# Candidates moved by a two-scalar operation, and a tile's eight diagonal matrices of maxima made in one product

## The chip, the core and the metric

The kernel runs on one core of a Trainium2 chip. A core has TensorE (matrix products, with its weight loads shown apart), VectorE, ScalarE, GpSimd and SyncE (which issues most of the DMAs), each with a program of its own; they meet at semaphores only. The metric is the device time of one execution in microseconds (us), lower being better.

## The reference, cut to what matters

One layer of a streaming encoder runs over 2048 prompt frames and 32 sample frames. Each frame is normalised and projected; half of the projection goes through a pooling mixer, the other half through sparse attention with 8 query heads of 64 on 2 key heads. For every query an indexer scores all visible keys, the 256 best are kept, and softmax attention runs over those:

```python
score = jnp.where(vis[None], score, -jnp.inf)
_, sel = lax.top_k(score, topk)
...
logits = jnp.einsum('bqgrd,bqkgd->bqgrk', qg, ks) * ATTN_SCALE + bias
p = jax.nn.softmax(logits, axis=-1)
```

Both halves are gated, projected out, normalised and added to the input.

## The kernel before, in words

The queries are cut into 17 tiles of 128 (16 of the prompt, the last with the 32 sample frames). The kernel has two phases, one after the other. `phase1` makes the projections, the pooling and the index scores, from a list of steps that all engines walk through. `phase2` is the attention: step t of its loop holds the logits and the weighted values of tile t, the maxima of the logits of tile t+1, the search for a later tile, and the output projection of tile t-2. `pe_step`, `dve_step` and `act_step` merge these series into one order for each engine by given fractions of a step.

**The search.** The 256th best score of each query is found by halving an interval, not by sorting. A query has its own partition and its own candidate `cand`, a column of 128 x 1. A round (`halve`, lines 336 to 355) has three VectorE instructions, each waiting for the one before it: count the scores that reach the candidate (L345, as wide as the tile has keys; it reads the candidate as a scalar per partition), compare the count with 256 and scale the answer to 0 or the width of the interval (L349, one column), and move the candidate (L352, one column). Tiles 2 to 5 are searched in the first phase, 26 rounds each (104). For tiles 6 to 16 ScalarE does 16 rounds in the second phase and VectorE the other 10 (110). Lists of scores are searched one at a time here, so each call has a single candidate column.

**The diagonals.** For each tile, TensorE multiplies queries and keys, and VectorE takes the maximum of each row and head (`maximum`, L1711). `set_shift` (lines 1714 to 1722) turns the eight negated maxima of a query, `nmax`, into eight diagonal matrices in bf16, `shift`: the identity, each row scaled by that query's value, one instruction a head (L1721). TensorE adds them to the logits by a product with ones (L1618), so the first logits of a tile wait for `shift_done`. GpSimd multiplies the exponentials of the nearer keys by the bias (L1501) in the meantime, and ScalarE makes those exponentials (L1576).

After `set_shift` VectorE goes on with `choose` (lines 358 to 386), which makes the mask of a later tile.

Of the kernel before, what the change touches and what calls it, by code (L numbers as in the profile page):

```python
# [16 lines left out]
ALU = mybir.AluOpType  # L17
# [9 lines left out]
P = 128  # L27
# [11 lines left out]
NH, HD, NKV, GRP = 8, 64, 2, 4  # L39
# [37 lines left out]
def key_tiles(t):  # L77
    return t + 1 if t < NPT else PAST // P + 1
# [236 lines left out]
def half_width(r):  # L315
    return 2.0 ** -r
# [9 lines left out]
def recentre(dve, done, n, B, scores):  # L326
    m = len(scores)
    dve.wait_ge(done, n)
    for i, s in enumerate(scores):
        dve.tensor_scalar(s, s, B.cand[:, i:i + 1], None, ALU.subtract).then_inc(done, 1)  # L330
    dve.wait_ge(done, n + m)
    dve.memset(B.cand[:, 0:m], 0.0).then_inc(done, 1)
    return n + m + 1


def halve(dve, done, n, B, scores, first, last):


    m = len(scores)
    for r in range(first, last):  # L340
        if r == ZOOM_AT:
            n = recentre(dve, done, n, B, scores)
        dve.wait_ge(done, n)
        for i, s in enumerate(scores):
            dve.tensor_scalar((B.above, B.reach)[i][:, 0:s.shape[1]], s, B.cand[:, i:i + 1], None,  # L345
                              ALU.is_ge, ALU.add, accum_out=B.cnt[:, i:i + 1]).then_inc(done, 1)
        n += m
        dve.wait_ge(done, n)
        dve.tensor_scalar(B.side[:, 0:m], B.cnt[:, 0:m], TOPK - 0.5, 2.0 * half_width(r), ALU.is_ge, ALU.mult)\  # L349
           .then_inc(done, 1)  # L350
        dve.wait_ge(done, n + 1)
        dve.scalar_tensor_tensor(B.cand[:, 0:m], B.side[:, 0:m], half_width(r), B.cand[:, 0:m], ALU.subtract, ALU.add)\  # L352
           .then_inc(done, 1)
        n += 2
    return n


def choose(dve, done, n, B, i, s):


    def link(ins):
        nonlocal n
        ins.then_inc(done, 1)
        n += 1

    half = half_width(ALL_ROUNDS - 1)
    col = slice(i, i + 1)
    w = s.shape[1]
    dve.wait_ge(done, n)
    link(dve.tensor_scalar(B.lo[:, col], B.cand[:, col], half, None, ALU.subtract))  # L370
    link(dve.tensor_scalar(B.hi[:, col], B.cand[:, col], half, None, ALU.add))
    dve.wait_ge(done, n)
    link(dve.tensor_scalar(B.above[:, 0:w], s, B.hi[:, col], None, ALU.is_gt, ALU.add, accum_out=B.cnt[:, col]))
    link(dve.tensor_scalar(B.reach[:, 0:w], s, B.lo[:, col], None, ALU.is_ge))
    dve.wait_ge(done, n)

    link(dve.tensor_scalar(B.room[:, col], B.cnt[:, col], -1.0, float(TOPK), ALU.mult, ALU.add))

    link(dve.tensor_tensor_scan(s, B.reach[:, 0:w], B.above[:, 0:w], 0.0, ALU.add, ALU.subtract))  # L379
    link(dve.tensor_tensor(B.above[:, 0:w], B.reach[:, 0:w], B.above[:, 0:w], ALU.add))  # L380
    dve.wait_ge(done, n)

    link(dve.scalar_tensor_tensor(B.reach[:, 0:w], s, B.room[:, col], B.above[:, 0:w],  # L383
                                  ALU.is_gt, ALU.is_ge))
    dve.wait_ge(done, n)
    return n
# [830 lines left out]
def phase2(nc, A, sb, sem, identf, identb, onesb, k2, home, loaded, unit, xs, first_q, banks, wide, q_dram, gb_dram, ma_dram,  # L1217
           s_dram, m_dram, g_dram, k_dram):

    def chunks(t):  # L1220
        n = key_tiles(t) * P
        return [(a, min(a + 512, n)) for a in range(0, n, 512)]
# [24 lines left out]
    def last_fl(t, kv=NKV - 1):  # L1247
        return fl[t, kv, key_tiles(t) - 1]
# [17 lines left out]
    def sslot(t):  # L1266
        return (t - FIRST) % 3
# [36 lines left out]
    with ExitStack() as st:  # L1304
# [7 lines left out]
        B = Search(sb, st, 1, SEQ)  # L1312
# [12 lines left out]
        shift = sb(st, "shift", [P, 2, NH, P], BF16)  # L1325
# [5 lines left out]
        nmax = sb(st, "nmax", [P, NH], F32)  # L1331
# [25 lines left out]
        shift_done = sem("shift_done")  # L1357
# [9 lines left out]
        with nc.Block() as block:  # L1367
# [301 lines left out]
            @block.vector  # L1669
            def _(dve):  # L1670
                n = 0

                def link(ins):
                    nonlocal n
                    ins.then_inc(dk, 1)
                    n += 1

                def continue_search(u):

                    nonlocal n  # L1680
                    dve.wait_ge(halved, HALVED * (u - FIRST + 1))
                    dve.tensor_scalar(B.cand[:], minus_cand[:, u % 2:u % 2 + 1], -1.0, None, ALU.mult)\
                       .then_inc(cand_taken, 1)
                    dve.wait_ge(cand_taken, u - FIRST + 1)

                def set_mask(u):
                    nonlocal n
                    w = key_tiles(u) * P
                    if u > FIRST:
                        dve.wait_ge(mask_done, u - FIRST)  # L1690
                    n = choose(dve, dk, n, B, 0, S[sslot(u)][:, 0:w])
                    dve.wait_ge(fl_full, last_fl(u - 3) + 1)
                    dve.tensor_scalar(mask[:, u % 3, 0:w], B.reach[:, 0:w], MASKED, None, ALU.mult)\
                       .then_inc(mask_done, 1)
                    dve.memset(B.room[:], 0.0).then_inc(S_used, 1)

                def maximum(t, h, c):

                    if h == 0 and c == 0:
                        if t < TOPK // P:  # L1700
                            dve.wait_ge(plain_mask, 2 * (t + 1))
                        elif t in EARLY:
                            dve.wait_ge(mask_in[t % 3], 16 * ((t - EARLY[0]) // 3 + 1))
                        else:
                            dve.wait_ge(mask_done, t - FIRST + 1)
                    k = fx[t, h, c]
                    a, b = chunks(t)[c]
                    dve.wait_ge(fx_full, k + 1)
                    if k >= 2:
                        dve.wait_ge(fx_free, k - 1)  # L1710
                    dve.tensor_tensor_reduce(junk[:, k % 2, 0:b - a], max_banks[k % 3][:, 0:b - a], mask[:, t % 3, a:b],  # L1711
                                             1.0, LEAST, ALU.add, ALU.max, mxp[:, h, c:c + 1]).then_inc(fx_free, 1)

                def set_shift(t):
                    dve.wait_ge(fx_free, last_fx(t) + 1)
                    link(dve.tensor_reduce(nmax[:], mxp[:, :, 0:len(chunks(t))], AX.X, ALU.max, negate=True))
                    dve.wait_ge(dk, n)
                    if t >= 2:
                        dve.wait_ge(fl_full, last_fl(t - 2) + 1)
                    for h in range(NH):  # L1720
                        ins = dve.tensor_scalar(shift[:, t % 2, h, :], identb[:], nmax[:, h:h + 1], None, ALU.mult)  # L1721
                    ins.then_inc(shift_done, 1)

                def invert_sums(t):
                    dve.wait_ge(sums_out, 4 * (t + 1))
                    n = GRP * queries(t)
                    dve.reciprocal(den[:, t % 2, 0:n], den[:, t % 2, 0:n]).then_inc(recip_done, 1)  # L1727

                def post_norm(t):
                    nonlocal n  # L1730
                    dve.wait_ge(o_free, 4 * (t + 1))
                    link(dve.tensor_tensor(root[:, 3:4], ss2[:, t, 0:1], ss2[:, t, 1:2], ALU.add))
                    dve.wait_ge(dk, n)
                    n = inverse_root(dve, dk, n, root[:, 0:1], root[:, 1:2], root[:, 2:3], root[:, 3:4], 1.0 / D)
                    dve.wait_ge(gpost_in, 16)
                    dve.scalar_tensor_tensor(osb[:, t % 2], osb[:, t % 2], root[:, 1:2], gpost[:], ALU.mult, ALU.mult)\
                       .then_inc(post_done, 1)

                for t in range(-1, NT + 3):
                    for kind, *at in dve_step(t):  # L1740
                        if kind == "R":
                            u, r = at
                            if r == ZOOM_AT:
                                continue_search(u)
                            n = halve(dve, dk, n, B, [S[sslot(u)][:, 0:key_tiles(u) * P]], r, r + 1)
                        elif kind == "M":
                            maximum(*at)
                        elif kind == "S":
                            set_shift(*at)
                        elif kind == "I":  # L1750
                            invert_sums(*at)
                        elif kind == "P":
                            post_norm(*at)
                        else:
                            set_mask(*at)
# [72 lines left out]
```

## Time and profile before

| | us |
|---|---|
| median of 3 runs | 1680.02 |
| lowest and highest of them | 1678.92, 1682.78 |
| span of the profiled execution | 1677.7 |
| TensorE busy | 1556.8 |
| VectorE busy | 1214.6 |
| ScalarE busy | 892.7 |
| GpSimd busy | 474.5 |

The span is the time from the first to the last instruction of one profiled execution; that execution's time is given by its span alone, and the median stands beside it. Busy times are of whole engines over the whole span, so they hide that the two phases have different limits.

### The profile page before, as it was taken

The page shows a single profiled execution, that of the slowest core. Times are in us where ns is not written, and L with a number is a line of the kernel's source. Part 1 is how long each engine was busy: PE and PEld are TensorE (multiplying, and loading weights), DVE is VectorE, ACT ScalarE, POOL GpSimd, SP SyncE. Part 2 cuts the span into 40 slices and gives each one's busy share as a digit, 9 for nine tenths or more (in the row PEclk, how much of TensorE's full clock was granted, in tenths as well). Part 3 has the DMA queues.
Part 4 walks back from the last instruction along what each step waited for, and adds up shares of the span by engine and source line. Part 5 has one row for each costly group of instructions (what it writes and reads, how often), then busy time and mean ns, then how long its engine had stood idle before and what let it go on. Part 6 is the DMA issues. An engine that isn't in the chain of part 4 may idle for free.

```text
span 1677.7 us, 17799 instructions
## 1 busy us (share of the span) xinstructions
PE 1556.8 (93%) x5191; PEld 869.7 (52%) x5191; DVE 1214.6 (72%) x2940; ACT 892.7 (53%) x1684; POOL 474.5 (28%) x384
## 2 busy tenths in 40 slices
PE   7999899989999999896988898999999999999996
PEld 4555555555555887663444444444444444455552
DVE  5412578779897566675469999999998999985322
ACT  3112333343334455451498988898988776523331
POOL 0111211121113132303343443434323342322241
PEclk9999999989999999987998999999999999999999
DMA  9322322221112111078324211221220220201011
GB/s 366 74 42 49 80 61 71 56 82 40 61 42 70 48 50 37 35 222 253 81 63 120 80 50 57 59 85 39 61 76 26 52 63 1 63 25 26 32 34 49
DMA packets 91979, 120.76 MB, mean 72 GB/s; under 512 B 17150, under 2 KB 63806, under 8 KB 91499
## 3 DMA queue, kind: packets, MB, share of 16 engines
q1 hardware_dynamic: 90506, 115.44, 22.1%
q10 hardware_dynamic: 1376, 4.19, 2.2%
q8 instruction: 42, 0.69, 0.2%
q14 instruction: 55, 0.44, 0.1%
HBM read 76.06 MB, written 43.54 MB: 71 GB/s over the span
## 4 chain that ended last, share of the span: by engine, by line
PE 23%; DVE 18%; ACT 6%; issue 5%; POOL 2%; POOLq 0%; DVEq 0%; ACTq 0%
PE wide L1648 7%; PE wide L1633 7%; DVE above L345 6%; DVE max_junk L1711 3%; ACT act_junk L1542 2%; PE bank L1613 2%; PE bank L1614 2%; PE bank L1615 2%; PE bank L1618 2%; POOL E L1501 1%; PE bank L1599 1%; DVE den L1727 1%; ACT E L1576 1%; DVE reach L383 1%; DVE S L379 1%
## 5 line engine op out<-in xcount | busy, mean ns | idle before, releaser
L931 PE MATMUL bank<-hT,home 128*128 128x512 f32 (+2 forms) x1280 | 486.1, 516 | 5.1 <-DVE sga L1145 2.4
L1501 POOL TENSOR_TENSOR E<-E,home 128x512 f32<-128x512 f32 (+1 forms) x174 | 251.9, 1452 | 446.8 <-ACT E L1576 446.7
L931 PEld LDWEIGHTS bank<-hT,home 128*128 128x128 f32 x1280 | 234.8, 191 | 165.1 <-issue 144.0
L1576 ACT ACTIVATE E<-bank 128x512 f32<-128x512 f32 (+1 forms) x290 | 165.5, 571 | 245.1 <-PE bank L1618 243.3
L1633 PE MATMUL wide<-E,home 128*128 128x512 f32 x544 | 285.1, 606 | 9.9 <-POOL E L1501 9.7
L907 ACT ACTIVATE relu<-wide 128x1024 f32<-128x1024 f32 (+7 forms) x192 | 153.9, 802 | 216.7 <-PE wide L949 154.5
L1183 DVE SCALAR_TENSOR_TENSOR S<-relu,wi,S 128x1024 f32<-128x1024 f32 (+7 forms) x168 | 173.7, 1034 | 100.1 <-ACT relu L907 92.6
L1711 DVE CUSTOM_DVE_ANT_0 max_junk<-bank,mask 128x512 bf16<-128x512 f32 (+3 forms) x230 | 136.9, 615 | 69.2 <-PE bank L1599 54.6
L1648 PE MATMUL wide<-home 128*128 128x512 f32 x272 | 142.2, 614 | 23.2 <-ACT osb L1568 23.0
L1542 ACT ACTIVATE act_junk<-S,minus_cand 128x1152 bf16<-128x1152 f32 (+5 forms) x105 | 155.4, 1480 | 1.5
L949 PE MATMUL wide<-kiT,qiT 96*128 96x512 f32 (+3 forms) x304 | 139.4, 527 | 6.6 <-ACT relu L907 6.5
L931 PE MATMUL bank<-home,hT 128*128 128x296 f32 (+1 forms) x544 | 141.0, 405 | 2.5 <-ACT hT L815 2.5
L1648 PE MATMUL wide<-home,yT 128*128 128x512 f32 x272 | 135.8, 593 | 0.0
L1633 PEld LDWEIGHTS wide<-E,home 128*128 128x128 f32 x544 | 104.4, 194 | 55.6 <-POOL E L1501 17.6
L744 POOL TENSOR_TENSOR win<-U 128x512 f32<-128x512 f32 (+11 forms) x20 | 22.6, 1129 | 347.9 <-ACT U L851 347.9
L931 PEld LDWEIGHTS bank<-home,hT 128*128 128x128 f32 x544 | 104.7, 195 | 30.6 <-ACT hT L815 4.4
L345 DVE TENSOR_SCALAR_CACHE_REDUCE above<-S,search 128x1152 bf16<-128x1152 f32 (+5 forms) x70 | 118.6, 1694 | 0.5
L1615 PE MATMUL bank<-identb,mask 128*128 128x512 bf16 (+1 forms) x290 | 112.8, 389 | 0.0
L1613 PE MATMUL bank<-first_q,k 128*128 128x512 f32 x182 | 107.5, 591 | 5.0 <-issue 2.9
L1618 PE MATMUL bank<-shift,onesb 128*128 128x512 bf16 (+1 forms) x290 | 109.6, 378 | 0.0
L1599 PE MATMUL bank<-k,first_q 128*128 128x512 f32 (+3 forms) x145 | 91.5, 656 | 14.6 <-DVE mxp L1711 9.8
L1711 DVE CUSTOM_DVE_ANT_0 max_junk<-wide,mask 128x512 bf16<-128x512 f32 (+3 forms) x114 | 65.4, 574 | 38.9 <-PE wide L1599 21.4
(204 smaller groups left out, 2392.2 us busy)
## 6 DMA issues: line engine op xcount, KB each, us to landing
xs<-x_prompt SPq DMA_DIRECT2D x16, 512.0 KB, 4.5
home<-w_in SPq DMA_DIRECT2D x16, 512.0 KB, 12.8
xr<-x_prompt SPq DMA_DIRECT2D x16, 512.0 KB, 4.2
y_prompt<-osb SPq DMA_DIRECT2D x16, 512.0 KB, 2.9
first_q<-q_high_scratch SPq DMA_DIRECT2D x24, 256.0 KB, 5.0
s_scratch<-S SPq DMA_DIRECT2D x11, 512.0 KB, 2.7
first_q<-q_low_scratch SPq DMA_DIRECT2D x18, 256.0 KB, 4.2
gb<-gb_scratch SPq DMA_DIRECT2D x17, 256.0 KB, 5.3
```

Source lines behind the costliest of these rows:

```text
L345: dve.tensor_scalar((B.above, B.reach)[i][:, 0:s.shape[1]], s, B.cand[:, i:i + 1], None, ALU.is_ge, ALU.add, accum_out=B.cnt[:, i:i + 1]). ...
L907: act.activation(relu[:, k % 2, 0:b - a], wide[k % 2][:, 0:b - a], ACT.Relu)\
L931: mm = pe.matmul(out, stationary(c), moving(c), start=(c == 0), stop=(c == DC - 1))
L1183: dve.scalar_tensor_tensor(row, relu[:, k % 2, 0:b - a], w, row, ALU.mult, ALU.add)\
L1501: pool.tensor_tensor(E[:, k % 4, :, 0:n], E[:, k % 4, :, 0:n], EB[:, kv * GRP:(kv + 1) * GRP, off:off + n], ALU.mult)\
L1542: act.activation(act_junk[:, 0:w], S[sslot(u)][:, 0:w], ACT.Sign, bias=minus_cand[:, u % 2:u % 2 + 1], accum_out=act_sum[:])\
L1576: act.activation(E[:, k % 4, :, 0:n], banks[2 + k % 2][:, 0:GRP * n].rearrange("p (j n) -> p j n", j=GRP), ACT.Exp).then_inc(fl_free, 1)
L1615: pe.matmul(bank, mask[:, t % 3, kt * P:(kt + 1) * P], identb[:, 0:n].rearrange("p (a n) -> p a n", a=1).broadcast_to([P, GRP, n]), start= ...
L1618: pe.matmul(bank, onesb[:], shift[:, t % 2, kv * GRP:(kv + 1) * GRP, 0:n], start=False, stop=True)\
L1633: pe.matmul(wide[0][:, kv * 512:kv * 512 + GRP * n].rearrange("p (j n) -> p j n", j=GRP), values[:, kt, kv:kv + 2, :].rearrange("p a d -> ...
L1648: mm = pe.matmul(wide[1][:, 0:512], stat, wout[:, c, i * 512:(i + 1) * 512], start=(c == 0), stop=(c == DC - 1))
L1711: dve.tensor_tensor_reduce(junk[:, k % 2, 0:b - a], max_banks[k % 3][:, 0:b - a], mask[:, t % 3, a:b], 1.0, LEAST, ALU.add, ALU.max, mxp[: ...
```

## The change

In a round of the search, the instruction that moves the candidate, (side - half) + candidate, reads two tensors, `side` and `cand`. It becomes a `tensor_scalar` that reads one tensor, `side`, adds the candidate as a scalar per partition, and subtracts the half width as an immediate; one instruction for each candidate column, of which there is one. The order of the two additions changes; the count of instructions and waits does not.

In `set_shift`, the eight scalings of the identity become one `tensor_tensor` product of 128 x 1024: the identity repeated over the heads, times the maxima repeated over the columns.

```diff
@@ -349,9 +349,10 @@
         dve.tensor_scalar(B.side[:, 0:m], B.cnt[:, 0:m], TOPK - 0.5, 2.0 * half_width(r), ALU.is_ge, ALU.mult)\
            .then_inc(done, 1)
         dve.wait_ge(done, n + 1)
-        dve.scalar_tensor_tensor(B.cand[:, 0:m], B.side[:, 0:m], half_width(r), B.cand[:, 0:m], ALU.subtract, ALU.add)\
-           .then_inc(done, 1)
-        n += 2
+        for i in range(m):
+            dve.tensor_scalar(B.cand[:, i:i + 1], B.side[:, i:i + 1], B.cand[:, i:i + 1], half_width(r), ALU.add, ALU.subtract)\
+               .then_inc(done, 1)
+        n += 1 + m
     return n
 
 
@@ -1717,9 +1718,9 @@
                     dve.wait_ge(dk, n)
                     if t >= 2:
                         dve.wait_ge(fl_full, last_fl(t - 2) + 1)
-                    for h in range(NH):
-                        ins = dve.tensor_scalar(shift[:, t % 2, h, :], identb[:], nmax[:, h:h + 1], None, ALU.mult)
-                    ins.then_inc(shift_done, 1)
+                    dve.tensor_tensor(shift[:, t % 2], identb[:].rearrange("p (a n) -> p a n", a=1).broadcast_to([P, NH, P]),
+                                      nmax[:].rearrange("p (h a) -> p h a", a=1).broadcast_to([P, NH, P]), ALU.mult)\
+                       .then_inc(shift_done, 1)
```

## Rows read from the trace of the kernel before

**Rows 1.** The page's first line: the span.
```profile
span 1677.7 us, 17799 instructions
```
**Rows 2.** Who TensorE waited for, 180 to 520 us: us in total, times, longest.
```profile
...
PE bank L1004 <- DVE xs L1069: 0.6, 1, 0.6
...
```
**Rows 3.** Busy us of each engine (xinstructions) by stretch; TensorE's granted clock.
```profile
core 0: us, PE busy (x) PEld busy (x) DVE busy (x) ACT busy (x) POOL busy (x), PEclk, DMA share, GB/s
...
957.00:1302.00 345.00, 318.91 (x994) 156.96 (x993) 330.03 (x748) 299.14 (x552) 133.34 (x88) 0.99 0.19 57
1302.00:1530.00 228.00, 214.43 (x695) 107.30 (x694) 207.56 (x427) 132.25 (x244) 79.64 (x45) 1.00 0.14 38
...
```
**Rows 4.** Who TensorE waited for, 957 to 1302 us.
```profile
PE bank L1599 <- DVE mxp L1711: 13.0, 10, 2.7
...
PE wide L1599 <- DVE mxp L1711: 4.9, 3, 2.7
PE wide L1633 <- POOL E L1501: 2.8, 4, 1.2
```
**Rows 5.** Who TensorE waited for, 1302 to 1530 us.
```profile
PE wide L1633 <- POOL E L1501: 6.7, 6, 1.7
PE bank L1599 <- DVE mxp L1711: 3.6, 5, 1.1
PE wide L1599 <- DVE mxp L1711: 3.1, 4, 2.0
```
**Rows 6.** Two lines of a round: shortest/median/longest ns, first and last start us.
```profile
L352 DVE SCALAR_TENSOR_TENSOR search<-search,search x214: 158/159/1445, 183.6 to 1516.9; 128x1 f32<-128x1 f32 x107
...
L349 DVE TENSOR_SCALAR search<-search x214: 153/153/156, 183.4 to 1516.7; 128x1 f32<-128x1 f32 x107
```
**Rows 7.** Timeline of VectorE and GpSimd, 1195 to 1205 us: start, duration, instruction.
```profile
1198.62 1.02 DVE L352 SCALAR_TENSOR_TENSOR search<-search,search 128x1 f32<-128x1 f32 x1
...
1202.95 0.16 DVE L352 SCALAR_TENSOR_TENSOR search<-search,search 128x1 f32<-128x1 f32 x1
...
1198.34 1.28 POOL L1501 TENSOR_TENSOR E<-E,home 128x512 f32<-128x512 f32 x1 [1.19 <-ACT E L1576]
```
**Rows 8.** Busy us of L352 alone by stretch, with its count.
```profile
180.00:520.00 340.00, 24.87 (x104) 0.98 0.22 61
768.00:957.00 189.00, 7.17 (x20) 0.91 0.42 121
957.00:1302.00 345.00, 18.39 (x60) 0.99 0.19 57
1302.00:1530.00 228.00, 8.43 (x30) 1.00 0.14 38
```
**Rows 9.** L345 in 1178 to 1224 us; two groups of VectorE: busy us, mean ns.
```profile
L345 DVE TENSOR_SCALAR_CACHE_REDUCE above<-home,search x10: 1933/1943/1947, 1178.4 to 1220.2; 128x1664 bf16<-128x1664 f32 x10
...
L1069 DVE TENSOR_SCALAR xs<-xs,small 128x1024 f32<-128x1024 f32 x17 | 12.8, 753 | 0.6
...
L1078 DVE TENSOR_SCALAR home<-home,gpre 128x552 f32<-128x552 f32 x8 | 3.8, 504 | 0.7 <-DMA home<-w_in 0.7
```
**Rows 10.** Timeline of VectorE and GpSimd at three tiles' diagonals.
```profile
1518.56 1.39 DVE L1721 TENSOR_SCALAR shift<-identb,nmax 128x128 bf16<-128x128 bf16 x8
...
1293.82 2.42 DVE L1721 TENSOR_SCALAR shift<-identb,nmax 128x128 bf16<-128x128 bf16 x8 [0.25 <-DVE nmax L1716]
...
1294.25 1.29 POOL L1501 TENSOR_TENSOR E<-E,home 128x512 f32<-128x512 f32 x1 [1.73 <-ACT E L1576]
...
1224.06 2.32 DVE L1721 TENSOR_SCALAR shift<-identb,nmax 128x128 bf16<-128x128 bf16 x8
```
**Rows 11.** Busy us of L1721 alone by stretch, with its count.
```profile
957.00:1302.00 345.00, 13.34 (x48) 0.99 0.19 57
1302.00:1530.00 228.00, 6.14 (x24) 1.00 0.14 38
```
**Rows 12.** A product of 1024 columns on VectorE: busy us, mean ns.
```profile
L1084 DVE TENSOR_TENSOR home<-home,gpre 128x1024 f32<-128x1024 f32 x16 | 18.7, 1215 | 0.0
```
**Rows 13.** Timeline of VectorE and GpSimd, and the chain of waits, 790 to 800 us.
```profile
792.12 4.26 DVE L1721 TENSOR_SCALAR shift<-identb,nmax 128x128 bf16<-128x128 bf16 x8
...
791.81 3.70 POOL L1501 TENSOR_TENSOR E<-E,home 128x512 f32<-128x512 f32 x3
...
795.20 1.28 issue
```

## The prediction

> **What bounds the kernel now.** I read the page first, then the busy time by stretch, then the waits of TensorE in each stretch, and last the two lines of the change in the timeline beside GpSimd. The span is 1677.7 us [rows 1]; the median of the runs shown is 1680.02 us, so 2.3 us lie around the span, and I add them at the end.
>
> The span falls into parts. Up to 768 us runs the projection phase, where TensorE sets the pace: in 180 to 520 us, which holds all 104 search rounds of that phase, it waited for VectorE only once, for 0.6 us [rows 2]. From 768 us on the attention phase runs. In its middle, 957 to 1302 us, VectorE is busy 330.03 of 345 us and TensorE 318.91 [rows 3]. TensorE therefore stands still for 26.1 us there, and 13.0 + 4.9 = 17.9 us of that are waits for VectorE's maxima [rows 4]: VectorE is the bound and TensorE is close behind it. In 1302 to 1530 us TensorE stands still for 13.6 of 228 us [rows 3], 6.7 us of it for VectorE and 6.7 us for GpSimd's bias product [rows 5]. From 957 to 1530 us nine tiles' diagonals and 90 search rounds are made (60 and 30 by stretch); between 768 and 957 us there are 20 rounds, while ScalarE does its own half of the first searches.
>
> **The candidate's step.** Of the 214 executions of L352 half take 0.159 us, but the longest takes 1.445 us. The comparison just ahead of it, L349, has the same one column and takes 0.153 to 0.156 us in all 214 [rows 6]. The timeline says why: the L352 at 1198.62 us lasts 1.02 us and ends at 1199.64, just as the GpSimd product of 1198.34 + 1.28 us ends; the L352 at 1202.95 us meets no GpSimd work and takes 0.16 us [rows 7]. L352 reads two tensors from SBUF and stands until GpSimd has finished; L349 reads one and never stands. What this standing is worth follows by stretch [rows 8]: 18.39 - 60 x 0.159 = 8.85 us in 957 to 1302; 8.43 - 30 x 0.159 = 3.66 us in 1302 to 1530; 24.87 - 104 x 0.159 = 8.33 us in the projection phase.
>
> The new instruction reads one tensor, and the candidate as a scalar per partition. No row shows this form at one column. What bounds it: L345 reads the same candidate the same way, at 1933 to 1947 ns for ten executions of one tile, so that read alone stands for nothing [rows 9]. As to duration, two one-tensor operations with such a scalar take 753 ns at 1024 columns and 504 ns at 552, that is 0.5275 ns a column, which leaves 504 - 551 x 0.5275 = 213 ns at one column [rows 9]. That is 0.054 us over L352's 0.159 us. It is the upper end; the lower end is nothing, where the instruction behind starts before this one has ended. In the attention phase mostly a maximum follows that does not wait for the candidate, so I take 0.03 us a round, between the two: 1.8 us in the middle stretch (0 to 3.2) and 0.9 us in the later one (0 to 1.6). In the projection phase the next comparison often waits for the candidate, so up to 104 x 0.054 = 5.6 us of the 8.3 us go back. Whatever is left there I cost at nothing: TensorE's projections cover it, and all that could come back is the 0.6 us of [rows 2]. If that cover were gone, the 2.7 us would be paid out in full.
>
> **The diagonals.** Eight instructions undisturbed take 1.39 us (the tile at 1518.56). At 1293.82 they take 2.42 us, and GpSimd's product starts only at 1294.25, behind the first of them: it gets in between two of the eight. At 1224.06 they take 2.32 us, with the standing ahead of the first [rows 10]. In the middle stretch 13.34 - 6 x 1.39 = 5.0 us are standing [rows 11]. Two of its six tiles are of the first sort (at 994.82 and 1293.82, 2.1 us), four of the other (2.9 us). One product reads two tensors, so the 2.9 us ahead of it stay; nothing can get into the middle of it, so the 2.1 us go. Its own price has a close row: a product of two f32 tensors of 1024 columns, one of them broadcast along its inner dimension, takes 1.215 us on the mean [rows 12]. That is 0.175 us less than the eight. Saved in the middle stretch: 6 x 0.175 + 2.1 = 3.1 us, or 1.05 us if the standing only moves ahead. In the later stretch, 6.14 - 3 x 1.39 = 1.97 us are standing [rows 11], 1.03 us of it in the middle of the eight (at 1365.16): saved 3 x 0.175 + 1.03 = 1.56 us, at least 0.53.
>
> A rule of the Trainium skill speaks against this part: VectorE: DVE Perf Modes, section "The TRN2 errata", gives 58 cycles plus the columns over the mode's factor at 0.96 GHz, by which eight narrow scalings in the fourfold mode would be an estimated 0.75 us and one product at the single rate 1.13 us, dearer by 0.38 us a tile. By that the whole would come to 1672.6 us. The trace disagrees on the eight, 1.39 us, so I go by the rows.
>
> One tile more counts. At 792.12 us the eight take 4.26 us, since GpSimd has three products in a row and two of them get in between [rows 13]. One product would stand for the first alone (0.92 us) and be done 4.26 - 0.92 - 1.215 = 2.1 us sooner. The chain has 1.28 us there in which TensorE does nothing [rows 13], because its logits wait for this diagonal. I take 1.3 us (0 to 2.1). In the rest of 768 to 957 us I take nothing: ScalarE's comparisons cover it, and without that cover 7.17 - 20 x 0.159 = 4.0 us would be there [rows 8].
>
> **The sum.** Middle stretch: 8.85 - 1.8 + 3.1 = 10.15 us off VectorE. Of TensorE's idle time there 17.9 of 26.1 us are waits for VectorE, so I count 0.7: 7.1 us. Later stretch: 3.66 - 0.9 + 1.56 = 4.3 us, and 6.7 of 13.6 us make it 0.5: 2.2 us. With 1.3 us at 792, 10.6 us. 1677.7 - 10.6 + 2.3 = 1669.4 us. What is late next is TensorE itself, and behind it GpSimd's products. If all came through at the best ends, it would be 11.95 + 5.2 + 2.1 + 0.6 = 19.9 us, or 1660 us.
>
> **Rivals.**
> A: The new one-column step stands for GpSimd like the old. Then it brings no gain and costs its 0.03 us: (3.1 - 1.8) x 0.7 + (1.56 - 0.9) x 0.5 + 1.3 = 2.5 us, 1677.5 us. For it: the diagonals read one tensor as well, and they stand [rows 10]. Against it: L349, one column, and L345, the same scalar, never do [rows 6, 9]. Chance 0.06. The Trainium skill puts it so (GPSIMD Engine Reference, section "Key points"): GpSimd contends with VectorE instructions in a two-port mode or with two SBUF inputs; whether one column counts as such a mode it doesn't say, and L349 says no.
>
> B: The freed time is taken up by TensorE, busy 318.91 of 345 us [rows 3], and by ScalarE, busy 299.14. If 0.2 of it comes through and nothing at 792: 0.2 x (10.15 + 4.3) = 2.9 us, 1677.1 us. Against it: the 17.9 us of waits on VectorE [rows 4]. Chance 0.13.
>
> C: The product is dearer than the eight. Its second operand is broadcast; if that halves the rate of its row, it takes 1.215 us less a fixed 0.159, doubled, plus 0.159, which is 2.27 us, 0.88 us over the eight. Then (8.85 - 1.8 + 2.1 - 5.3) x 0.7 + (3.66 - 0.9 + 1.03 - 2.6) x 0.5 + 1.1 = 4.4 us, 1675.6 us. Against it: the row has such a broadcast too [rows 12]. Chance 0.05.
>
> D, the other side: GpSimd is kept out. Today it gets in after one of the eight; behind the product its bias products come late by up to 1.215 us, and TensorE's weighted values wait for them (2.8 and 6.7 us now [rows 4, 5]). If that hits all nine tiles from 957 us on and all of it reaches TensorE, it costs 10.9 us against the candidate step's (8.85 - 1.8) x 0.7 + (3.66 - 0.9) x 0.5 = 6.3 us: 1684.6 us. It decides from eight of the nine tiles on. Against it: only three of those nine tiles have GpSimd coming in behind the start. Chance 0.04.
>
> **How the numbers follow.** The forecast has 0.72; its own range is 1663 to 1676 us. Within 0.2% (3.4 us, about what a measurement of this kernel can tell from no change) lie A, most of B and a little of the forecast: 0.19. Slower is D: 0.04. Faster has the rest, 0.77. For 8 in 10 the range reaches from 1662, short of the best ends, to 1678, which takes in A, B and C.
>
> **What would show it.** L352 at about 0.16 to 0.22 us in all 214, none near 1 us. L1721 once a tile, 1.2 us or 1.2 us plus one standing. VectorE's busy time down by some 20 to 30 us in all. TensorE's waits for the maxima in the middle stretch down from 17.9 to under 12 us. The forecast is wrong if L352 still shows 1 us records, if TensorE's busy share goes past 97% in the middle with the span unmoved, or if its waits for GpSimd's products grow by several us. A lower granted clock than the 0.99 of that stretch [rows 3] would hide the gain too.

## The result, and the profile after

The median fell from 1680.14 to 1661.53 us (4 runs each); the ratio is 0.9889 with a 95% interval of 0.9875 to 0.9903. The forecast was 1669.4 us and a range of 1662 to 1678 us, so the direction came out, the time lies 0.5 us below the range, and the gain of 18.6 us is 1.75 times the 10.6 us forecast. The profiled execution has a span of 1660.2 us, 17.5 us less than before.

Two of the first lines of the page of the changed kernel, to set beside [rows 1]; the second has the busy time and the count of instructions of each engine:

```profile
span 1660.2 us, 17680 instructions
...
PE 1553.8 (94%) x5191; PEld 871.6 (52%) x5191; DVE 1190.2 (72%) x2821; ACT 892.4 (54%) x1684; POOL 481.3 (29%) x384
```

The 119 instructions that are gone are the seven scalings saved at each of the 17 tiles. VectorE is busy 24.4 us less, TensorE 3 us less.

The candidate's step and the diagonals of the changed kernel, and last the eight scalings of the kernel before; shortest/median/longest ns, beside [rows 6] and [rows 10]:

```profile
L353 DVE TENSOR_SCALAR search<-search,search x214: 212/214/216, 182.9 to 1499.4; 128x1 f32<-128x1 f32 x107
...
L1721 DVE TENSOR_TENSOR shift<-identb,nmax x17: 1224/1226/2224, 769.9 to 1574.9; 128x1024 bf16<-128x1024 bf16 x17
...
L1721 DVE TENSOR_SCALAR shift<-identb,nmax x136: 235/245/1376, 767.9 to 1593.4; 128x128 bf16<-128x128 bf16 x136
```

None of the 214 candidate steps stands any more: the longest takes 0.216 us where it took 1.445. In the timelines 29 of the 110 new steps of the attention phase lie wholly inside one GpSimd instruction and take no longer for it; of the old ones none did. The product takes 1.224 us, and up to 2.2 us with standing ahead of it.

To see where the time came from I cut both traces at the starts of `nmax`, the reduction just ahead of each tile's diagonals, so a stretch runs from one tile's `nmax` to a later one's. The start of tile 0's is also the border of the two phases. The lines of both kernels by stretch (busy us of each engine, then TensorE's granted clock); of the kernel before first, the phases and four stretches of the attention phase:

```profile
0.00:767.70 767.70, 724.55 (x2571) 456.20 (x2571) 501.41 (x1284) 284.82 (x509) 141.27 (x159) 0.98 0.28 83
767.70:1677.70 910.00, 832.20 (x2620) 413.51 (x2620) 713.17 (x1657) 607.92 (x1175) 333.21 (x226) 0.97 0.22 63
...
855.00:898.80 43.80, 38.68 (x111) 18.65 (x110) 33.44 (x99) 39.53 (x89) 16.64 (x13) 0.92 0.29 79
898.80:945.30 46.50, 42.13 (x125) 20.30 (x125) 44.85 (x110) 44.09 (x94) 21.22 (x16) 0.96 0.32 91
...
945.00:1293.00 348.00, 321.72 (x1004) 158.38 (x1004) 333.18 (x749) 303.00 (x562) 135.17 (x87) 0.99 0.21 61
1293.00:1518.00 225.00, 211.43 (x684) 105.60 (x683) 204.42 (x426) 137.07 (x254) 76.12 (x44) 1.00 0.14 38
```

And the same of the changed kernel:

```profile
0.00:769.70 769.70, 729.74 (x2571) 460.70 (x2571) 498.64 (x1283) 285.26 (x509) 141.40 (x159) 0.97 0.28 83
769.70:1660.20 890.50, 824.05 (x2620) 410.88 (x2620) 691.59 (x1538) 607.13 (x1175) 339.93 (x226) 0.98 0.22 64
...
854.40:895.80 41.40, 36.04 (x114) 17.70 (x114) 31.85 (x92) 39.64 (x90) 17.02 (x13) 1.00 0.26 70
895.80:939.50 43.70, 38.99 (x120) 18.99 (x118) 42.23 (x102) 42.25 (x91) 19.76 (x16) 1.00 0.38 109
...
939.70:1277.00 337.30, 319.19 (x1006) 157.22 (x1005) 323.06 (x708) 303.85 (x562) 138.59 (x88) 0.99 0.22 63
1277.00:1501.00 224.00, 212.62 (x685) 106.59 (x684) 199.91 (x405) 136.65 (x254) 79.25 (x44) 0.99 0.14 38
```

The projection phase is 2.0 us longer, the attention phase 19.5 us shorter (910.0 to 890.5). Of those 19.5 us, 2.3 come between the diagonals of tiles 4 and 5 (43.8 to 41.4), 2.8 in the next stretch (46.5 to 43.7), 10.6 in the six tiles behind it (348.1 to 337.5, a little wider than the windows shown) and 1.1 in the three after (225.0 to 223.9); 2.5 us more come at the tile of 792 us (28.6 to 26.1 between its `nmax` and the next). VectorE's busy time in the six tiles falls from 333.18 to 323.06, by 10.1 us: there the run became shorter by about as much as VectorE was relieved. TensorE's busy time in the attention phase fell too, from 832.20 to 824.05 us for the same 2620 instructions, at a granted clock of 0.98 after 0.97; how much of the gain goes with that is taken up at the single tiles below.

### The profile page after: what moved, and what is told of

Its sections match the earlier page's. It is cut to its first block, busy times and chain, and to the rows that moved or that the text cites. A ratio compares the mean times of both kernels' runs of the same rounds, so it can differ in the third digit from the quotient of the medians.

```text
span 1660.2 us, 17680 instructions
## 1 busy us (share of the span) xinstructions
PE 1553.8 (94%) x5191; PEld 871.6 (52%) x5191; DVE 1190.2 (72%) x2821; ACT 892.4 (54%) x1684; POOL 481.3 (29%) x384
## 4 chain that ended last, share of the span: by engine, by line
PE 23%; DVE 20%; issue 6%; ACT 3%; POOL 2%; POOLq 0%; DVEq 0%; ACTq 0%
PE wide L1649 7%; DVE above L345 7%; PE wide L1634 7%; DVE max_junk L1712 3%; PE bank L1614 2%; PE bank L1615 2%; PE bank L1616 2%; PE bank L1619 2%; DVE den L1728 2%; POOL E L1502 2%; PE bank L1600 1%; ACT act_junk L1543 1%; DVE reach L384 1%; DVE S L380 1%; DVE above L381 1%
## 5 line engine op out<-in xcount | busy, mean ns | idle before, releaser
L1502 POOL TENSOR_TENSOR E<-E,home 128x512 f32<-128x512 f32 (+1 forms) x174 | 258.6, 1491 | 423.6 <-ACT E L1577 423.6
L1649 PE MATMUL wide<-home 128*128 128x512 f32 x272 | 140.0, 605 | 24.1 <-ACT osb L1569 23.9
L932 PE MATMUL bank<-home,hT 128*128 128x296 f32 (+1 forms) x544 | 144.6, 413 | 2.5 <-ACT hT L816 2.5
L345 DVE TENSOR_SCALAR_CACHE_REDUCE above<-S,search 128x1152 bf16<-128x1152 f32 (+5 forms) x70 | 118.6, 1695 | 0.5
L1600 PE MATMUL bank<-k,first_q 128*128 128x512 f32 (+3 forms) x145 | 92.3, 661 | 10.6 <-DVE mxp L1712 5.8
```

The lines of the kernel that those rows point to most:

```text
L932: mm = pe.matmul(out, stationary(c), moving(c), start=(c == 0), stop=(c == DC - 1))
L1502: pool.tensor_tensor(E[:, k % 4, :, 0:n], E[:, k % 4, :, 0:n], EB[:, kv * GRP:(kv + 1) * GRP, off:off + n], ALU.mult)\
L1649: mm = pe.matmul(wide[1][:, 0:512], stat, wout[:, c, i * 512:(i + 1) * 512], start=(c == 0), stop=(c == DC - 1))
```

## The experiments

Three things were open: what each part is worth, whether GpSimd is the cause, and why more came through than the shares of the prediction allow. "S" in the expectations stands for the theory that VectorE is saturated from 899 to 1365 us, "P" for the prediction's shares. In the table, "attention" is the time from the first `nmax` to the end in each profiled execution, and "eight tiles" the stretch from the `nmax` of tile 5 (898.76 us in the kernel before) to that of tile 13 (1364.94 us).

| kernel | median us | ratio to before, 95% interval | attention us | eight tiles: length, VectorE busy us |
|---|---|---|---|---|
| before | 1680.1 | | 910.0 | 466.2, 446.6 |
| changed | 1661.5 | 0.9889 (0.9875 to 0.9903) | 890.5 | 451.3, 432.0 |
| candidate only | 1668.5 | 0.9928 (0.9916 to 0.9941) | 897.8 | 455.7, 434.1 |
| product only | 1669.4 | 0.9926 (0.9914 to 0.9939) | 898.3 | 458.4, 440.5 |
| first 20 rounds old | 1663.1 | 0.9890 (0.9875 to 0.9904) | 892.5 | 453.1, 434.0 |
| projection rounds old | 1661.6 | 0.9884 (0.9869 to 0.9899) | 890.7 | 451.3, 432.0 |
| extra, one tensor | 1670.8 | 0.9944 (0.9929 to 0.9959) | 899.6 | 459.2, 441.6 |
| extra, two tensors | 1673.6 | 0.9959 (0.9945 to 0.9974) | 902.5 | 464.8, 447.8 |
| before, bias cut | 1640.7 | 0.9755 (0.9736 to 0.9774) | 868.7 | 436.0, 415.2 |
| changed, bias cut | 1633.9 | 0.9725 (0.9710 to 0.9739) | 863.8 | 432.9, 408.7 |
| reciprocal cut | 1648.7 | 0.9804 (0.9784 to 0.9824) | 879.2 | 443.5, 411.0 |

The kernel before had a median of 1682.0 us beside the first four experiments, 1680.3 beside the next four and 1679.6 beside the last, so ratios are safer to compare than medians. The lengths from the traces repeat better still in the one pair that should agree: the changed kernel and the one with the old rounds in the projection phase are 0.2 us apart in the attention phase.

**Each part alone.** The candidate's step alone, in the kernel before:

```diff
-        dve.scalar_tensor_tensor(B.cand[:, 0:m], B.side[:, 0:m], half_width(r), B.cand[:, 0:m], ALU.subtract, ALU.add)\
+        for i in range(m):
+            dve.tensor_scalar(B.cand[:, i:i + 1], B.side[:, i:i + 1], B.cand[:, i:i + 1], half_width(r), ALU.add, ALU.subtract)\
```

> Only the candidate's step is changed; the eight scalings stay. Theory S (saturation): from the tile of 899 us to that of 1365 us VectorE never stands idle, so what comes off it there shortens the run one for one. The standing of L352 in those 80 rounds is 13.1 us and the scalar costs some 2 us back: 11 to 12 us faster than before, about 1668.5 us. Theory P (the prediction's shares: nothing before 957 us, 0.7 to 1302, 0.5 after): 6.3 us faster, about 1674 us.

It is 12.1 us faster by its ratio (0.0072 x 1682), 12.2 us in the attention phase, and all 214 steps take 213 to 216 ns. P is refuted for this part. S has the sum, in part by luck: the eight tiles became 10.6 us shorter (466.2 to 455.6) for 12.5 us less of VectorE's busy time, and another 1.6 us lie between the `nmax` of tiles 3 and 4 (34.5 to 32.9), where no round runs; the granted clock was 1.00 there in this trace, and 0.95 before and in the changed kernel.

The product alone, in the kernel before (the second half of the diff of the change):

> Only the eight scalings are made one product; the candidate's step stays as before. S: 2.2 us at the tile of 792 us and some 5 us over the eight saturated tiles: 7 us faster than before, about 1673 us. P: 1.3 + 2.2 + 0.8 = 4.3 us faster, about 1676 us. If the two parts are independent, their gains add up to the change's 18.6 us.

It is 12.4 us faster by its ratio and 11.7 us in the attention phase: more than either theory said. The longest old candidate step there still takes 1.448 us. VectorE's busy time in the eight tiles falls by 6.1 us, while the instructions that write `shift` account for 3.8 of them; the steps of L352 account for another 1.8 although they were not touched. I read it so: where GpSimd's products meet VectorE's instructions depends on the timing of both, and moving one moves the other meetings. The parts do not add up: 12.2 + 11.7 = 23.9 us apart, 19.5 together in the attention phase. Of the 4.4 us between, 1.8 are this standing of L352, which both parts take away, and 1.6 are the stretch without rounds above; the rest is open, and so is why these eight tiles became 7.7 us shorter for 6.1 us of relief. My expectation priced the product's own instructions alone and missed this.

**Where the rounds matter.** The changed kernel with the old step in some rounds, first in those of tiles 6 and 7 (the first 20 of the attention phase):

```diff
+        if B.old:
+            dve.scalar_tensor_tensor(B.cand[:, 0:m], B.side[:, 0:m], half_width(r), B.cand[:, 0:m], ALU.subtract, ALU.add)\
+               .then_inc(done, 1)
...
                                 continue_search(u)
+                                B.old = u < FIRST + 2
```

> The changed kernel with the old candidate step in the first 20 rounds of the attention phase (tiles 6 and 7, between 855 and 945 us). P: ScalarE covers these rounds, so nothing changes: 1661.5 us, within 0.6. S: the second ten of them lie in the saturated part and some of the first ten too, so the standing of 4.0 us, less some 0.5 us for the scalar, comes back at least by half: 2 to 3.5 us slower than the changed kernel, 1664 us.

The timed ratio cannot tell it from the changed kernel. The trace can. Its lines for the stretches between the diagonals of tiles 4, 5 and 6, first of all engines, then of the 20 old steps alone:

```profile
853.70:896.20 42.50, 36.54 (x113) 17.65 (x114) 33.21 (x93) 40.73 (x91) 17.54 (x13) 1.00 0.27 71
896.20:942.80 46.60, 40.75 (x121) 19.05 (x122) 45.10 (x103) 42.86 (x91) 21.18 (x15) 1.00 0.35 100
...
853.80:896.20 42.40, 3.15 (x10) 1.00 0.27 71
896.20:942.80 46.60, 4.97 (x10) 1.00 0.35 100
```

The first ten rounds bring 1.0 us back (41.4 to 42.4), the second ten 2.9 us (43.7 to 46.6), which is their 4.97 us less the 2.14 us that ten new steps take. The granted clock is 1.00 in both stretches, as in the changed kernel, so it isn't the clock. The two kernels with one part each say the same of the second stretch, the candidate's step alone first, then the product alone:

```profile
897.93:941.68 43.75, 38.94 (x118) 19.02 (x118) 42.24 (x109) 42.30 (x91) 19.90 (x16) 1.00 0.38 109
```

```profile
896.49:943.10 46.61, 40.77 (x121) 19.08 (x122) 45.12 (x103) 42.86 (x91) 21.19 (x15) 1.00 0.35 101
```

The new step brings the whole 2.8 us there and the product nothing; the kernel before took 46.5 us at a clock of 0.96, the product alone 46.6 at 1.00. In later stretches 1.7 us are won again, why was not taken apart, and 2.0 us remain in the attention phase. The prediction had counted these rounds at nothing.

Then the old step in the 104 rounds of the projection phase:

> The changed kernel with the old candidate step in the 104 rounds of the projection phase. P and S: TensorE sets the pace there and nothing changes, 1661.5 us within 0.6. Rival: the projection phase pays for VectorE's standing too; the changed trace was 2.4 us ahead at 500 us, before it lost that again where the granted clock was lower; then it is 2 to 3 us slower, 1664 us.

The ratio is 0.9884 against 0.9889, and that phase takes 768.1 us against 769.7 us in the changed kernel: VectorE's standing there costs nothing that can be seen. The 2.0 us by which the changed kernel's projection phase was longer are not the rounds' doing: with the candidate's step alone that phase takes 768.2 us, with the product alone, and so the old rounds, 769.3. The changed kernel's granted clock is 0.97 in that stretch against 0.98 before; that this is the reason was not tried.

**Is it GpSimd?** The trace of the kernel before answers for most rounds that stood: 38 of the 214 executions of L352 take over 0.25 us, and 36 of them end within 0.03 us of the end of a GpSimd instruction, all 26 in the attention phase among them (the other two, in the projection phase, end 0.7 us ahead of one). Of these 26, 15 end with a bias product (7.7 us of standing), the other 11 with GpSimd's further work on the outputs (L1460, L1466 and L1473, 8.7 us). The test: GpSimd's bias product cut from 512 columns to 4, in both kernels (the bias is then left out for nearly all queries):

```diff
-                            pool.tensor_tensor(E[:, k % 4, :, 0:n], E[:, k % 4, :, 0:n],
-                                               EB[:, kv * GRP:(kv + 1) * GRP, off:off + n], ALU.mult)\
+                            pool.tensor_tensor(E[:, k % 4, :, 0:1], E[:, k % 4, :, 0:1],
+                                               EB[:, kv * GRP:(kv + 1) * GRP, off:off + 1], ALU.mult)\
```

> The kernel before, with GpSimd's bias product cut from 512 columns to 4 (the bias is left out for nearly all queries). GpSimd's work falls by some 200 us. If the standing is GpSimd's doing, L352 stands in the attention phase only for the products of the means and the residual, a third of the 16.5 us, and the eight scalings hardly; the kernel is faster than before by some 12 to 16 us, about 1667 us.

> The changed kernel with the same cut of GpSimd's bias product. If the change's gain is GpSimd's standing, it shrinks from 19 us to some 6 us or less (a third of the standing, 1.4 us of shorter diagonals, 0.8 us of scalars back): about 1661 us and less than 8 us under the kernel before with the same cut. If the gain came from shorter instructions or fewer of them, it stays near 19 us.

In the kernel before with this cut, L352 still takes up to 1.396 us, but in the attention phase its 110 executions stand for 8.6 us in all instead of 16.5:

```profile
L352 DVE SCALAR_TENSOR_TENSOR search<-search,search x214: 158/159/1396, 183.2 to 1479.9; 128x1 f32<-128x1 f32 x107
...
772.00:1640.70 868.70, 26.06 (x110) 0.98 0.23 66
```

(26.06 - 110 x 0.159 = 8.6.) Of its long executions there, 11 are left, and each ends with one of the three GpSimd lines that were not cut; none ends with a bias product. What the cut took away is what the bias product caused; the rest is half and not the third that I expected. The two kernels with the cut are 6.8 us apart (1640.66 and 1633.88), where the uncut ones are 18.6 us apart; in the attention phase 4.9 us against 19.5. That the gain shrinks has two reasons, though. Here are the eight tiles of the kernel before and of the changed one, both with the cut:

```profile
897.80:1333.80 436.00, 417.93 (x1340) 210.41 (x1338) 415.17 (x1000) 403.36 (x753) 80.03 (x116) 1.00 0.23 67
```

```profile
893.40:1326.30 432.90, 418.39 (x1342) 211.83 (x1341) 408.72 (x944) 403.61 (x754) 79.73 (x116) 1.00 0.23 66
```

The change relieves VectorE by 6.5 us where it was 14.6 without the cut, and of these only 3.1 come through; TensorE is as busy as VectorE there. So the standing is shown by which steps it left, and the gain of 4.9 us alone would not show it. That the cut kernel before gained 39 us, far more than the 12 to 16 expected, has a further reason that I left out: TensorE's waits for the products in the attention phase fall from the first line to the second (us in total, times, longest). That this makes up the whole difference is not shown.

```profile
PE wide L1633 <- POOL E L1501: 10.1, 12, 1.7
```

```profile
PE wide L1633 <- POOL E L1501: 1.2, 2, 1.0
```

**How much comes through.** The changed kernel with one instruction more in each of the 110 rounds of the attention phase, reading one tensor or two, its result not used:

```diff
+            dve.tensor_scalar(B.small[:], scores[0][:, 0:32], B.side[:, 0:1], None, ALU.is_ge, ALU.add,
+                              accum_out=B.extra[:]).then_inc(done, 1)
...
+            dve.scalar_tensor_tensor(B.extra[:], B.side[:, 0:1], 1.0, B.cnt[:, 0:1], ALU.subtract, ALU.add).then_inc(done, 1)
```

> The changed kernel with one more VectorE instruction in each of the 110 rounds of the attention phase: a count over 32 columns, one tensor, which should never stand for GpSimd; its result is not used. From the rows of the counts it takes 0.25 us a round. S: in the 80 rounds between the tiles of 899 and 1365 us each comes through whole, 20 us, in the other 30 little: 1661.5 + 20 to 23 = 1683 us. P: 0.25 x (60 x 0.7 + 30 x 0.5) = 14 us, 1676 us.

> The changed kernel with one more instruction in each of the 110 rounds of the attention phase: one column, two tensors, the form of the old candidate step; its result is not used. If the standing is GpSimd's, a quarter of them show up to 1.4 us again, 0.15 us a round on the mean beside 0.12 us each for the instruction. S: 80 x 0.27 = 21.6 us, about 1683 us. P: 0.27 x 57 = 15 us, 1677 us. If an extra instruction cost its 0.12 us alone: 9.6 us, 1671 us.

Their rows, of the first kernel and of the second:

```profile
L358 DVE TENSOR_SCALAR_CACHE_REDUCE extra_small<-S,search x70: 234/236/240, 908.3 to 1507.3; 128x32 bf16<-128x32 f32 x70
```

```profile
L358 DVE SCALAR_TENSOR_TENSOR extra<-search,search x110: 144/150/1301, 863.1 to 1511.2; 128x1 f32<-128x1 f32 x110
```

This one-tensor instruction never stands (0.240 us at most), the two-tensor one does (1.301 us), and its 24 records over 0.25 us all end within 0.03 us of a GpSimd instruction's end. Both totals (1670.8 and 1673.6 us) are below what S gave and below P too, so as forecasts both failed: I had priced each instruction by its record, and records overlap with their neighbours. The comparison by VectorE's busy time was made only afterwards: in the eight tiles it grew by 9.6 us and the stretch by 7.9 us, a share of 0.82, with one tensor; by 15.8 and 13.5 us, 0.85, with two. The prediction's shares make 0.59 on the mean over these 80 rounds (60 at 0.7, ten at 0.5, ten at nothing), so 0.82 and 0.85 are nearer to all than to that.

The other direction, a larger relief: VectorE's reciprocal of the sums on 32 columns instead of 512, which leaves the outputs of most queries unnormalised.

```diff
-                    dve.reciprocal(den[:, t % 2, 0:n], den[:, t % 2, 0:n]).then_inc(recip_done, 1)
+                    dve.reciprocal(den[:, t % 2, 0:32], den[:, t % 2, 0:32]).then_inc(recip_done, 1)
```

> The changed kernel with VectorE's reciprocal of the sums cut from 512 columns to 32 (the outputs are then not normalised for most queries). It takes some 3.1 us a tile off VectorE, 25 us over the eight saturated tiles, where TensorE stands still for 17 us in all in the changed kernel. S with VectorE as the only bound: 1661.5 - 25 to 28 = 1635 us. If TensorE takes over (rival B of the prediction, at a larger step): the first 8 to 15 us come through and the rest is lost, 1647 to 1653 us.

The eight tiles of this kernel, then of the changed one, then of the kernel before:

```profile
894.00:1337.50 443.50, 421.32 (x1317) 210.20 (x1341) 410.96 (x945) 404.26 (x754) 180.78 (x117) 1.00 0.22 65
```

```profile
895.70:1347.00 451.30, 425.01 (x1340) 209.30 (x1339) 431.96 (x946) 404.50 (x753) 183.41 (x117) 1.00 0.23 65
```

```profile
898.70:1364.90 466.20, 430.62 (x1343) 211.59 (x1341) 446.62 (x1002) 405.48 (x754) 178.69 (x117) 0.99 0.22 62
```

VectorE is relieved by 21.0 us, the stretch becomes 7.8 us shorter: 0.37. With TensorE at 421 and ScalarE at 404 of 443.5 us, VectorE (411) is no longer the busiest, and I read it so that the bound has passed from it. So the change's own relief of 14.6 us (446.6 to 432.0) came through whole, 14.9 us (466.2 to 451.3), and of the next 21 us, taken off at this place, 8 did. "Whole" is not exact: over the runs with VectorE as the busiest engine the share goes from 0.82 to 1.27 (the product alone).

## Why the prediction was too small

**Right.** The mechanism: the two-tensor step stands until a GpSimd instruction ends, the one-tensor step never does (rival A is refuted by 214 records of 212 to 216 ns). So VectorE and GpSimd, which the program joins at semaphores only, met in these instructions too. The number of tensors is not the whole of it: the eight scalings of the kernel before read one tensor, of 128 columns in bf16, and stood as well (1.376 us at the longest, where the median is 0.245). What sets them apart from the one-tensor step was not tried. The price of the new step, 213 ns from [rows 9], was met to 1 ns. The product's 1.215 us from [rows 12] came out at 1.224, so rival C fell, and with it the estimate by the Trainium skill (VectorE: DVE Perf Modes, "The TRN2 errata") that it would be dearer than the eight, which had taken 1.39 us and not the estimated 0.75. VectorE's relief was also sized right in sum: 10.1 us measured in the six tiles for 10.15 forecast in about that stretch, and 4.5 us (204.42 to 199.91) for 4.3 in the later one. Rival D did not show: TensorE's waits for GpSimd's product stayed at 2.3 and 7.3 us ([rows 4, 5]: 2.8 and 6.7), although GpSimd's busy time rose by 6.8 us (474.5 to 481.3), and at the tile of 792 us it was indeed held back, its three products taking 4.70 us instead of 3.70:

```profile
793.62 4.70 POOL L1502 TENSOR_TENSOR E<-E,home 128x512 f32<-128x512 f32 x3
...
793.92 2.04 DVE L1721 TENSOR_TENSOR shift<-identb,nmax 128x1024 bf16<-128x1024 bf16 x1
```

**Wrong: the steps that turn the relief into time.** In the attention phase I forecast 10.6 us and 19.5 came. The missing 8.9 us are: 3.5 in the middle stretch, 5.1 between 855 and 945 us, 1.2 at the tile of 792 us, and 0.2 before that, less 1.1 in the later stretch, where I had too much.

The step "of TensorE's idle time there 17.9 of 26.1 us are waits for VectorE, so I count 0.7" asked the wrong engine: 10.6 us came for 10.1 us of relief. What the runs point to instead is how much the relieved engine itself stands idle, and VectorE's own waits in that part were few. Its waits in the eight tiles of the kernel before (us in total, times, longest):

```profile
DVE max_junk L1711 <- PE bank L1599: 4.5, 8, 1.3
DVE max_junk L1711 <- PE wide L1599: 2.7, 3, 1.5
DVE shift L1721 <- DVE nmax L1716: 0.5, 2, 0.3
```

7.7 us in 466, with VectorE busy for 446.6: an engine that waits so little passes most of its relief on until another is as full, and TensorE was not yet (430.6 of 466.2 us). In the later stretch, 1293 to 1518 us, the same list comes to 15.8 us, and of 4.5 us of relief only 1.1 came, where the share of 0.5 had 2.2.

The step "in the rest of 768 to 957 us I take nothing: ScalarE's comparisons cover it" cost most of the 5.1 us: 3.9 of them came back with the 20 old rounds. I had cut the stretch at 957, where the chain of waits changes from ScalarE to VectorE, and so averaged one saturated tile with idle ones. Between 899 and 945 us the chain of the kernel before is ScalarE's and TensorE's, and yet VectorE's whole list of waits is one line:

```profile
by line: ACT act_junk L1542 20.4%; PE wide L1648 15.4%; PE wide L1633 13.1%; issue 10.1%; ACT E L1576 6.9%; ACT act_search L1550 5.2%; ACT minus_cand L1557 4.1%; PE bank L1615 3.5%; PE bank L1614 3.5%; PE bank L1613 3.4%; PE bank L1618 3.3%
```

```profile
DVE max_junk L1711 <- PE bank L1599: 0.2, 1, 0.2
```

VectorE was nearly without a pause there (44.85 of 46.5 us busy), and the longest lines of the chain did not name it. The kernel with the first 20 rounds old shows that VectorE's standing costs its full price in this stretch. It does so in the stretch before it too, 1.0 us for ten rounds, although VectorE waited 7.8 us for ScalarE's candidate there; so a nearly empty list of waits is not a necessary condition. Why ScalarE did not cover it is argued, not shown: its comparisons are queued in order behind exponentials that wait for logits, which wait for VectorE's diagonals.

At 792 us I took the 1.28 us in which TensorE did nothing, and the 2.1 us that VectorE would be done sooner as the upper end; 2.5 us came. That tile's stretch, before and after:

```profile
791.91:820.51 28.60, 26.46 (x68) 12.00 (x68) 13.14 (x26) 7.95 (x15) 12.32 (x10) 0.85 0.34 94
```

```profile
793.72:819.83 26.11, 25.25 (x68) 11.82 (x68) 10.92 (x19) 7.95 (x15) 13.31 (x10) 0.90 0.38 108
```

TensorE's idle time fell from 2.14 to 0.86 us, by the 1.3 us forecast. The other 1.2 us are TensorE's busy time for the same 68 instructions, at a granted clock of 0.90 after 0.85. The stretch took 26.1 us at 0.90 with the product alone and 28.6 us at 0.85 with the candidate's step alone, so both parts of the gain go with the product; the prediction had no term for the clock, and why it was higher was not taken apart. Of the change between the diagonals of tiles 4 and 5, 1.0 us is the rounds'. The other 1.3 us go with the product. Alone it brings that stretch to 42.4 us, as in the kernel with the first 20 rounds old, and the candidate's step alone leaves it at 43.9. The granted clock is 0.92 before, 0.96 with the step alone and 1.00 with the product alone, so how much of this is the clock's is open.

Rival B, that the freed time is taken up, fails for this change and holds beyond it, as the cut reciprocal shows. No experiment that does all the work beat the changed kernel by more than the noise.

## What to carry to other kernels

In this kernel relief on an engine came through nearly whole (shares of 0.82 and more) where that engine's own list of waits was nearly empty and no other was as busy; read it tile by tile, because a stretch that mixes idle and saturated tiles hides it, and so does a chain whose longest lines name only one of two saturated engines. An instruction whose longest record is nine times its median, with a neighbour of the same size that never varies, is likely to be standing for something: look at what ends when it ends. Here it was GpSimd, and for this step of one column one tensor operand fewer avoided it, though the new instruction is a third longer.

## What the runs showed that was not expected

Two changes against the same contention did not add up: 12.2 and 11.7 us apart, 19.5 together, and the product alone took 1.8 us of standing off instructions that it had not touched. A measured instruction can cost less than its record where neighbours overlap: the 80 extra counts in the eight tiles have records of 19.6 us in all and raised VectorE's busy time by 9.6 us; 1.8 us of the difference are less standing of the product in that run (12.7 to 10.9 us). TensorE's granted clock was not the same from kernel to kernel at the start of the attention phase: the stretch between the `nmax` of tiles 3 and 4, where no round runs, took 34.5 us at 0.95 in the kernel before and the changed one, and 32.9 us at 1.00 in the one with the candidate's step alone.
